# Hybrid encoder block on one core: in mixer A, three of four query tiles of every second head turned in 32 by 32 blocks by VectorE and moved by transfers within SBUF; in mixer B, each pass's first unit reordered

## The reference

```python
h = rms_norm(x, norm1_g)
qa, ka, va, qb, kb, vb, ga, gb = split(h @ w_in)
ya = axial_gqa_attention(qa, ka, va) @ w_o_a     # mixer A: 8 query heads, 2 key heads, softmax over 512 keys
yb = dilated_window_attention(qb, kb, vb) @ w_o_b  # mixer B: 3 window groups x 4 heads, ALiBi
x = x + (sigmoid(ga + b) * ya + sigmoid(gb + b) * yb) @ w_out
x = x + expert_choice_swiglu(rms_norm(x, norm2_g), w_router, w_gate, w_up, w_down)
return rms_norm(x, normf_g)
```

## Time and profile before

| | us |
|---|---|
| median of 3 runs | 862.12 (861.91 to 864.86) |
| the profiled execution, its own time | 861.86 |
| its span, first to last instruction | 859.8 |
| PE busy | 839.4 (98%) |
| DVE busy | 379.3 (44%) |
| ACT busy | 264.1 (31%) |
| matmuls of the expert stage L1657, L1689 | 221.9 and 95.8 |
| mean granted TensorE clock | 0.998 |

### The profile page before, as it was taken

The page is one execution under the profiler, slowest core; times in us unless marked ns, Lnnn a source line. Parts: engine busy times, 40 slices in busy tenths (PEclk is TensorE's granted clock), DMA queues, the critical chain, the costliest instruction groups (busy, mean ns, idle before and its releaser), DMA issues.

```text
span 859.8 us, 10399 instructions
## 1 busy us (share of the span) xinstructions
PE 839.4 (98%) x4197; PEld 513.2 (60%) x4197; DVE 379.3 (44%) x665; ACT 264.1 (31%) x461; POOL 29.0 (3%) x50
## 2 busy tenths in 40 slices
PE   9999999999999999999999999999999998989996
PEld 8898866687878888888534343344433433334343
DVE  6377987797715254427322237223131321321351
ACT  6333876695624233216011010010100101001231
POOL 1050000000000000003000000000000000000010
PEclk9999999999999999999999999999999999999999
DMA  9830112023034234884899999999999999999996
GB/s 285 179 98 2 50 50 98 25 76 109 20 123 143 84 107 144 311 356 180 331 410 425 429 428 426 429 428 427 428 428 427 426 430 428 426 423 429 427 420 265
DMA packets 81490, 239.19 MB, mean 278 GB/s; under 512 B 8102, under 2 KB 63526, under 8 KB 65828
## 3 DMA queue, kind: packets, MB, share of 16 engines
q1 hardware_dynamic: 76016, 235.94, 69.7%
q10 hardware_dynamic: 5284, 2.09, 1.0%
q0 software_dynamic: 144, 0.51, 0.1%
HBM read 235.92 MB, written 2.62 MB: 277 GB/s over the span
## 4 chain that ended last, share of the span: by engine, by line
PE 88%; DMA 8%; DVE 1%; ACT 1%; issue 1%; POOLq 0%; POOL 0%; SPq 0%; DVEq 0%; ACTq 0%
PE psum L1657 21%; PE psum L1169 11%; PE psum L1689 11%; PE psum L1171 11%; PE psum L1170 11%; DMA wslot<-in_w_down 7%; PE psum L1614 3%; PE psum L1708 3%; PE psum L1357 2%; PE psum L1818 2%; PE psum L1326 2%; PE psum L1369 1%; PE psum L1669 1%; PE psum L1175 1%; PE psum L1622 1%; PE psum L1379 1%
## 5 line engine op out<-in xcount | busy, mean ns | idle before, releaser
L1657 PE MATMUL psum<-wslot,xinT 128*64 128x512 f32 x1000 | 221.9, 595 | 3.7 <-DMA wslot<-in_w_up 1.9
L1657 PEld LDWEIGHTS psum<-wslot,xinT 128*64 128x64 f32 x1000 | 69.5, 137 | 141.3 <-issue 131.8
L1689 PE MATMUL psum<-wslot,actT 128*64 128x512 f32 x424 | 95.8, 596 | 4.5 <-DMA wslot<-in_w_down 4.5
L1169 PE MATMUL psum<-hT_hi,w_hi 128*128 128x512 f32 x208 | 82.4, 396 | 0.9 <-DVE oT_lo L1991 0.9
L1170 PE MATMUL psum<-hT_lo,w_hi 128*128 128x512 f32 x208 | 81.2, 390 | 0.0
L1171 PE MATMUL psum<-hT_hi,w_lo 128*128 128x512 f32 x208 | 81.2, 390 | 0.0
L1892 DVE TENSOR_TENSOR w_lo<-w_raw,w_hi 128x1024 fp32r<-128x1024 f32 (+1 forms) x46 | 52.9, 1174 | 44.4 <-ACT w_hi L805 44.3
L1689 PEld LDWEIGHTS psum<-wslot,actT 128*64 128x64 f32 x424 | 29.4, 137 | 60.4 <-issue 58.0
L1101 ACT ACTIVATE actT<-psum 128x512 f32<-128x512 f32 x16 | 9.6, 597 | 171.2 <-PE psum L1669 171.2
L2305 DVE TENSOR_TENSOR x<-x,psum 128x512 f32<-128x512 f32 x48 | 29.7, 681 | 57.0 <-PE psum L1708 57.0
L2295 DVE TENSOR_TENSOR y_lo<-psum,y_hi 64x512 fp32r<-64x512 f32 x28 | 19.3, 689 | 80.4 <-ACT y_hi L1111 80.0
(11 more groups left out here) (285 smaller groups left out, 1306.5 us busy)
## 6 DMA issues: line engine op xcount, KB each, us to landing
wslot<-in_w_up SPq DMA_DIRECT2D x24, 2048.0 KB, 25.0
wslot<-in_w_gate SPq DMA_DIRECT2D x24, 2048.0 KB, 23.9
wslot<-in_w_down SPq DMA_DIRECT2D x22, 2048.0 KB, 22.4
w_raw<-in_w_in SPq DMA_DIRECT2D x34, 512.0 KB, 4.7
wslot<-in_w_up SPq DMA_DIRECT2D x15, 1024.0 KB, 11.0
wslot<-in_w_down SPq DMA_DIRECT2D x15, 1024.0 KB, 27.5
wslot<-in_w_gate SPq DMA_DIRECT2D x14, 1024.0 KB, 11.2
w_raw<-in_w_out SPq DMA_DIRECT2D x8, 512.0 KB, 4.9
```

What stands on the lines that cost most here:

```text
L1169: pe.matmul(out_, s_hi, m_hi, start=(k == 0), stop=False)
L1657: mm = pe.matmul(bank[2 * e + n][CAP * f:CAP * f + CAP, :], xinT[:, HALF * h + k, CAP * e:CAP * e + CAP], wslot[place_of(m)][:, k % PART, ...
L1689: mm = pe.matmul(bank[4 + e][CAP * f:CAP * f + CAP, :], actT[:, e, k, CAP * h:CAP * h + CAP], wslot[place_of(m)][:, k % PART, SEQ * f:SEQ ...
```

## The change

- Twelve units of mixer A, tiles 0, 1 and 2 of heads 0, 2, 4 and 6 (`in_blocks`: units 0 to 2, 8 to 10, 16 to 18, 24 to 26), aren't turned by PE. DVE gives only their reciprocal; ACT scales them (`scale_probs`), DVE turns each 32 x 32 block in place in its row of blocks (`turn_blocks`, written to the new buffer `blocks`), and SP moves the blocks of a head to their partitions in `pT` by 16 DMAs of 32 partitions x 4 x 96 elements, 48 KB each (`move_blocks`), put into the order of the strip loads ahead of strips 19, 20, 22 and 23. ACT no longer reads those units from PSUM.
- `pT` now has its columns in the order (query block of 32, tile, 32); `read_o` and `low_o` put them back.
- The values of heads 0 to 5 come one step later (`VALUES_AT` 10, 18, 26), and with them `O_READ` and `O_LOW`. `values_a` and the first turning of the next such head wait for `blocks_in`.
- In mixer B `turn_probs` of the first unit of each pass goes ahead of that unit's fill and its wait. The copy to `far` is made in step 33; unit 32 reads `dist` in its place.

```diff
+    blocks = sb("blocks", [NT, NT, 3 * SQ], 98)          # SQ = 32
...
+        def in_blocks(u):
+            return u < NA and u // NT % 2 == 0 and u % NT < NT - 1
...
+        def wait_blocks_in(eng, h):
+            eng.wait_ge(blocks_in, 16 * NT * NT * (h // 2 + 1))
...
-        O_READ, O_LOW = (10, 19, 26), (11, 21, NA)
+        VALUES_AT = (10, 18, 26)
+        O_READ, O_LOW = (11, 20, 27), (12, 22, NA)
...
+            def move_blocks(h):
+                sp.wait_ge(blocks_turned, blocks_before(NT * h + NT))
+                if h >= 2:
+                    sp.wait_ge(pv_done, h // 2)
+                for kq in range(NT):
+                    for q in range(NT):
+                        sp.dma_start(pT[SQ * kq:SQ * kq + SQ, 0, :, P * q:P * q + 3 * SQ],
+                                     blocks[SQ * q:SQ * q + SQ, :, kq, :]).then_inc(blocks_in, 16)
             for n in range(len(strips)):
+                if n in (19, 20, 22, 23):
+                    move_blocks(2 * (19, 20, 22, 23).index(n))
                 load_strip(n)
...
+            def scale_probs(u):
+                act_.wait_ge(probs_normed, u + 1)
+                p = probs_of(u)[:, 0:SEQ]
+                act_.activation(p, p, ACT.Copy, scale=column(rinv, u)).then_inc(probs_scaled, 1)
...
+                if u and in_blocks(u - 1):
+                    scale_probs(u - 1)
-                if 2 <= u < NA + 2:
+                if 2 <= u < NA + 2 and not in_blocks(u - 2):
                     read_probs(u - 2)
...
             def turn_probs(u):
+                if in_blocks(u):
+                    return
...
-                pe.wait_ge(pT_done, 2 * NT * (i + 1))
+                pe.wait_ge(pT_done, whole_before(2 * NT * (i + 1)))
+                wait_blocks_in(pe, 2 * i)
...
-                if u > 1 and u % (2 * NT) == 1:
-                    values_a(u // (2 * NT) - 1)
+                if u in VALUES_AT:
+                    values_a(VALUES_AT.index(u))
...
                     if u == first:
+                        turn_probs(u)
                         pe.wait_ge(o_lo_done, OA + hp)
                     fill(B_FILL[hp], u - first, todo)
...
-                    turn_probs(u)
+                    if u > first:
+                        turn_probs(u)
...
             def norm_probs(u, width):
                 dve.wait_ge(exp_done, u + 1)
+                if in_blocks(u):
+                    dve.reciprocal(column(rinv, u), column(rsum, u)).then_inc(probs_normed, 1)
+                    return
...
+            def turn_blocks(u):
+                head, c = divmod(u, NT)
+                if c == 0 and head >= 2:
+                    wait_blocks_in(dve, head - 2)
+                dve.wait_ge(probs_scaled, blocks_before(u + 1))
+                dve.transpose(blocks[:, :, :, SQ * c:SQ * c + SQ].rearrange("p k q s -> p (k q) s"),
+                              probs_of(u)[:, 0:SEQ].rearrange("p (b s) -> p b s", s=SQ)).then_inc(blocks_turned, 1)
...
                 if 1 <= u <= NA:
                     norm_probs(u - 1, SEQ)
+                if u >= 2 and in_blocks(u - 2):
+                    turn_blocks(u - 2)
...
-            settle(dve.tensor_copy(far[:, :], dist[:, 0, SEQ:SEQ + 2 * P]))
...
+                        if u == NA + 1:
+                            settle(dve.tensor_copy(far[:, :], dist[:, NT - 1, SEQ:SEQ + 2 * P]))
```

More of the change, by code:

```diff
@@ L56 @@
 KIB = 1024
+SQ = 32
 COL_A = 0
@@ L278, in encoder_block @@
         probs_turned = sem("probs_turned")
+        probs_scaled = sem("probs_scaled")
+        blocks_turned = sem("blocks_turned")
+        blocks_in = sem("blocks_in")
         pT_done = sem("pT_done")
@@ L392, in probs_of, with whole_before, blocks_before, turned_bank @@
             return (probs_a if u < NA else probs_b)[u % 3]
+        def in_blocks(u):
+            return u < NA and u // NT % 2 == 0 and u % NT < NT - 1
+        def whole_before(u):
+            return sum(not in_blocks(v) for v in range(u))
+        def blocks_before(u):
+            return u - whole_before(u)
+        def wait_blocks_in(eng, h):
+            eng.wait_ge(blocks_in, 16 * NT * NT * (h // 2 + 1))
         def wait_probs_free(eng, u):
             before = u - 3 if u < NA else max(u - 3, NA - 1)
-            if before >= 0:
-                eng.wait_ge(probs_turned, before + 1)
+            if before >= 0 and in_blocks(before):
+                eng.wait_ge(blocks_turned, blocks_before(before + 1))
+            elif before >= 0:
+                eng.wait_ge(probs_turned, whole_before(before + 1))
+        def turned_bank(u):
+            return tp[(0, 3)[whole_before(u) % 2]]
+        def token_order(i, rows):
+            if i >= OA:
+                return rows
+            return rows.rearrange("p (q c s) -> p c q s", q=NT, c=NT)
+        def by_tiles(i, rows):
+            if i >= OA:
+                return rows
+            return rows.rearrange("p (c q s) -> p c q s", q=NT, c=NT)
         def column(of, u):
@@ L899, in read_probs @@
                     act_.wait_ge(pv_done, head // 2)
-                act_.wait_ge(probs_turned, u + 1)
-                last = act_.activation(pT[:, head % 2, :, cols],
-                                       tp[(0, 3)[u % 2]][:, :].rearrange("p (k i) -> p k i", i=P), ACT.Copy)
+                act_.wait_ge(probs_turned, whole_before(u + 1))
+                if head < A_HEADS:
+                    dst = pT[:, head % 2, :, :].rearrange("p k (q c s) -> p k q c s", q=NT, c=NT)[:, :, :, c, :]
+                    src = turned_bank(u)[:, :].rearrange("p (k q s) -> p k q s", k=NT, q=NT)
+                else:
+                    dst = pT[:, head % 2, :, cols]
+                    src = turned_bank(u)[:, :].rearrange("p (k i) -> p k i", i=P)
+                last = act_.activation(dst, src, ACT.Copy)
                 if u >= NA:
@@ L906, in read_probs @@
                 last.then_inc(pT_done, 1)
+            def scale_probs(u):
+                act_.wait_ge(probs_normed, u + 1)
+                p = probs_of(u)[:, 0:SEQ]
+                act_.activation(p, p, ACT.Copy, scale=column(rinv, u)).then_inc(probs_scaled, 1)
             def read_o(i):
                 act_.wait_ge(pv_done, i + 1)
[L910 removed]
+                act_.activation(by_tiles(i, oT_hi[:, i, :]), token_order(i, tp[2][:, :]), ACT.Copy).then_inc(o_hi_done, 1)
             def high_col(g, hh):
@@ L1353, in turn_probs @@
                                      probs_of(u)[:, SEQ + P * g:SEQ + P * g + P], ident[:, :])
-                elif u >= 2:
-                    pe.wait_ge(pT_done, u - 1)
+                elif whole_before(u) >= 2:
+                    pe.wait_ge(pT_done, whole_before(u) - 1)
                 for k in range(NT):
-                    t = pe.transpose(tp[(0, 3)[u % 2]][:, P * k:P * k + P],
+                    t = pe.transpose(turned_bank(u)[:, P * k:P * k + P],
                                      probs_of(u)[:, P * k:P * k + P], ident[:, :])
```

24 lines of the change are left out of this document (12 added, 12 removed).

## The result

| | before | after |
|---|---|---|
| median | 862.19 us (861.91 to 864.86, 4 runs) | 874.05 us (872.7 to 875.67, 4 runs) |
| profiled execution, its own time | 861.86 | 875.67 |
| its span | 859.8 | 873.7 |
| ratio of the times | | 1.0128, 95% interval 1.011 to 1.0146 |

What follows compares the result with a forecast made beforehand. PE was taken to bound mixer A, with DVE not far, and the expert weight stream to set the end. Terms +0.5 - 2.8 + 0 + 0 + 1.7 = -0.6 took 861.86 to 861.3 us; range 857.8 to 867.5.

Steps and rivals of the forecast that it cites:

- the spacing of the issues in a row: Moves on SP: 16 DMAs issued one behind the other, 0.50 us apart, so a move takes 9.9 us.
- The first move: Mixer A's first values: the move lands at 110.55, PE waits 1.6 us; term +0.5 us.
- the reference point 110.07: Time in us when the kernel before reaches the same point of the program, without the 3.58 of the values.
- The second and third moves: Mixer A: each takes 9.9 us, the next values come some 18 us behind the previous ones, so both are hidden.
- the signs that the prediction named for being wrong: Moves over 12 us, transposes near 1.2 us, or no idle time in mixer B's second pass.
- The last move: Mixer A's fourth values: lands at V + 13.7, hidden with 0.6 us to spare; term 0.
- slack of 0.6 us: Time to spare between the last move's landing and the request for mixer A's fourth values.
- The transposes off PE: Mixer A: 12 units x 0.47 = 5.6 us off PE at most, only where PE stays the bound.
- the rival that gave it all: Mixer A: DVE becomes the bound, a transpose takes 1.2 us, the 2.8 gain is lost; 866.0 us, chance 0.12.
- First pass of mixer B: Reordering its first unit gains PE 0.7 us, given back at DVE's pace; bounds 0 and 0.7, term 0.
- Second pass: Mixer B: PE waits for DVE's scaling before its first unit's transposes, from 214.78 to 216.45; term +1.7 us.
- The transfers are slow: Rival on the moves: spacing 0.75 us, first move 3.8 later, last 3.2 beyond its slack; 869.9 us, chance 0.14.

Runs made afterwards that it cites:

- e6: The changed kernel with the first move issued ahead of strip 18's load instead of behind it; 870.84 us.
- e12: e9 with the moves issued from SP again, the first one ahead of strip 18's load; 862.51 us.
- e4: The changed kernel with the distance load in step 29 in place of 24; 868.88 us.
- e11: The kernel before with only its distance load issued in step 26 in place of 24; 862.38 us.
- e13: e12 with 4 of the last move's 16 transfers issued on ScalarE's queue; 862.03 us.
- e3: The changed kernel with each move as 4 transfers over 128 partitions, same bytes, blocks left on their own partitions so the output is wrong; 861.66 us.
- e2: The kernel before with only mixer B's reordering in both passes and the later copy to far; 865.02 us.
- e1: The changed kernel with the second pass of mixer B in the old order; 870.83 us.
- e9: The changed kernel with moves issued from GpSimd, distance load in step 26 and mixer B's second pass in the old order; 861.71 us.
- e5: The changed kernel with the 64 transfers of the four moves issued from GpSimd in place of SP; 867.51 us.
- e14: The kernel before plus 64 transfers of 48 KB from GpSimd that nobody needs; 865.97 us.
- e10: e9 with head 6 transposed by TensorE as before, so the last of the four moves is gone; 863.88 us.

## Why the prediction was wrong

The forecast failed at two steps above all: the spacing of the issues in a row, and the third and the last move counted as hidden, the third without a look at the load beside it. That PE pays for a wait twice, by the lower clock behind it, had no term at all.

- **The first move: +0.5 forecast, +4.6 measured** (112.85 net of the start against the reference point 110.07, and 1.77 in the values). Its start was right: 103.58 net of 2.65 is 100.93, against 100.65. PE was ready 0.6 late (scores ended at 112.2, 109.6 net, against 108.95). The step that failed is the *spacing*: 0.50 us was taken from issues of loads from HBM, between 0.46 and 0.55; it is 0.65. Over 15 issues that is 2.3 us. The landing, taken as 2.4, was 2.0. What followed was no term at all: behind 3.13 us of idle time PE runs at the lower clock and needs 1.77 more for the values. Starting the move earlier (e6) gives all 4.9 back; that the time fell by 3.2 only is the clock behind the fourth values.
- **The second and third moves, "hidden".** The second was. The third was not: it cost 5.1 us, and this is the largest miss. At 0.65 a move is 11.7 us long, still within the "some 18 us" between two values. But the distance load falls into its last third, and a landing of 6.0 in place of 2.0 put it past PE. Its issues, 1.25 us longer in all, took PE's last slack. The prediction looked at what is queued behind the moves on SP, and not at what else is on the 16 DMA engines, although the load's row (ACT's queue, step 24) is in the trace of before. With the load in step 26 (e12) PE doesn't wait there; e4 shows the wait going with the load to the next move, and e11 that it is the meeting, not the load. Of the signs that the prediction named for being wrong, this one came: the move lasted 16.9 us, over 12.
- **The last move: 0 forecast, 2.5 measured.** By the prediction's own slack of 0.6 us over 15 issues it is late from a spacing of 0.54 (the prediction says 0.60, which its sum doesn't give). e12 has it alone: 2.6 us of wait, which goes when 4 of the 16 issues go elsewhere (e13). 0.8 of such a wait comes back in mixer B.
- **The transposes off PE.** The forecast counted 5.6 us, 0.5 of it lost to DVE. With short moves (e3) mixer A and the first pass are 3.8 us shorter than before: DVE holds PE for 1.9, at the transposes of two of the first units and not between the values. DVE's transpose was 0.70 us, 0.65 forecast:

```profile
L2068 DVE STREAM_TRANSPOSE blocks<-probs_a x12: 684/703/712, 93.5 to 163.4; 128x512 f32<-128x512 f32 x12
```

  So VectorE took a third of the gain and no more, and the rival that gave it all fell. ("Some 18 us" between two values is 18.7 by the prediction's own terms; 17.9 and 18.6 were measured in e6 and e12.) The estimate of 1.24 us from the Trainium skill ("VectorE: DVE Perf Modes", section "The three transpose paths") doesn't hold for one instruction over 512 columns of 4-byte words; the measurement decides. ACT's scaling was 0.71 us for 0.59, hidden as said.
- **First pass of mixer B: 0.** Right (e2: its values start at 206.3).
- **Second pass: +1.7.** Right in place, cause and size (1.9 in the trace, 1.7 of it wait). What was missing is that such a wait can bring the lower clock behind it: 3.4 in e2's trace.
- **The right rival had too small a chance and the wrong reason.** "The transfers are slow" stood at 0.14, with a spacing of 0.75. With the measured 0.65 its own working gives some 4 us, 865, and not 874. Of the other 9 the distance load is 5.1 and the clock behind the first wait 1.8; the rest is spread over small parts (DVE's hold, 0.8 behind mixer B, up to 0.6 of the start) and isn't settled one by one. The Trainium skill's advice to batch ("DMA: Bandwidth & Descriptors", section "Measured (HBM→SBUF, 128 partitions, SWDGE, issued from GpSimd)") pointed the right way. What decides here, though, is the issuing engine's 0.65 us for each transfer, and not efficiency on the wire.

Two things stay open: why the end of the program takes 2.8 us more after 64 transfers from GpSimd, and what decides whether the clock falls behind a wait. The length of the wait alone doesn't: behind the second pass's 1.7 us it fell in e2 and e3 and not in the change, behind 3.1 us at the first values in the change and e1 and not in e4, behind 2.56 us at the last values in e6 and not in the change. So single differences of about 1.7 us between two of these kernels can be luck.

Of the versions that compute the whole layer none is clearly faster than the kernel before: e9, e12 and e13 are level with it.

## What to carry to other kernels

Count the transfers of a rearrangement before its bytes: in a row on one queue each costs 0.55 to 0.65 us here, whether it carries 48 or 192 KB, so a move of 16 on SP is a 12 us latency that must fit between producer and consumer on every occurrence, the first and the last most of all. Then look at what any other queue loads in the same time, and price a wait of TensorE of 1.7 us or more at one to two times its length (1.7 and 3.4 in the second pass, 3.1 and 4.9 at the first values). Work taken off the bounding engine (5.6 us of transposes, 3.8 won) is quickly paid back by one such wait.

## What the runs showed that was not expected

- A DMA of 48 KB within SBUF takes 0.60 us of SP, 0.63 of ACT and 0.55 of GpSimd to issue; it lands 1.9 to 2.2 us later as a rule (medians) and up to 7.5 beside a load of 1.5 MB.
- Behind a wait of TensorE for the values of 1.1 us or more, of which the traces hold fifteen, the sixteen matmuls ran in part at the lower clock level seven times (4.96 to 6.44 us in the timeline in place of 3.65): six of eight times behind 3.1 to 3.8 us, once of seven times behind 1.1 to 2.6. Behind the second pass's 1.7 us it was two of six times (0.85 for four transposes in place of 0.44).
- 64 transfers issued from GpSimd in the first 170 us make the end of the program 2.8 us longer (e5, e9, e14), 48 make it 1.8 longer (e10).
